# Two blocks on one core: VectorE takes the drain of the latent keys and the last nine low halves of the weights

## What is computed

```python
kvb = (rmsnorm(ckv, kv_a_norm[l]) @ w_kv_b[l]).reshape(B, S, N_HEADS_B, KV_HEAD_B)
k_nope, v_b = kvb[..., :QK_NOPE], kvb[..., QK_NOPE:]
...
x = x + rmsnorm(merged @ w_out[l], post_norm_mix[l])
h2 = rmsnorm(x, pre_norm_mlp[l])
y = jnp.square(jax.nn.relu(h2 @ w_up[l])) @ w_down[l]
x = x + rmsnorm(y, post_norm_mlp[l])
```

## Time and profile before

| | |
|---|---|
| runs, us | 1471.33, 1473.10, 1473.85; median 1473.1 |
| the profiled execution, us | 1473.38 |
| its span in the profile, us | 1471.5 |
| mean granted TensorE clock | 0.965 of full |
| busy: TensorE, VectorE, ScalarE, GpSimd | 90%, 65%, 34%, 34% |
| latent keys | 1097.0 to 1104.3 us of the span |
| up and down stage | about 1277 to 1459 us of the span |

### The profile page before, as it was taken

One profiled execution on the slowest core, in us unless ns is written; L12 is line 12 of the kernel. 1 busy time (PEld: TensorE's weight loads), 2 busy tenths in 40 slices (PEclk: granted clock), 3 DMA queues, 4 the chain that ended last, 5 costly groups with the idle time before them and its releaser, 6 DMA issues.

```text
span 1471.5 us, 25626 instructions
## 1 busy us (share of the span) xinstructions
PE 1317.9 (90%) x9926; PEld 1253.8 (85%) x9926; DVE 955.8 (65%) x2100; ACT 497.2 (34%) x974; POOL 496.9 (34%) x334
## 2 busy tenths in 40 slices
PE   6999999999998886887878886888899999989997
PEld 5999999989888886887868886878776889889997
DVE  4679987665658685859585859655325447683574
ACT  4633456444133121212112121211236455434341
POOL 1588722000224554453535353555012000022221
PEclk9999999999999999898999898999999999999998
DMA  6555554553488999999999999999830125245451
GB/s 244 212 188 185 176 187 166 184 177 154 165 343 329 426 427 427 428 427 427 428 426 426 426 427 427 427 428 427 337 143 29 58 86 194 94 157 199 160 191 40
DMA packets 58090, 397.43 MB, mean 270 GB/s; under 512 B 6288, under 2 KB 9872, under 8 KB 10384
## 3 DMA queue, kind: packets, MB, share of 16 engines
q0 software_dynamic: 36864, 268.45, 43.6%
q1 hardware_dynamic: 21136, 127.76, 24.3%
HBM read 395.14 MB, written 1.05 MB: 269 GB/s over the span
## 4 chain that ended last, share of the span: by engine, by line
PE 55%; DMA 20%; DVE 14%; issue 7%; ACT 3%; POOL 1%; DVEq 0%; POOLq 0%; ACTq 0%
DMA rows_late<-peer_uv_dram,stage 20%; PE bank L721 10%; PE bank L723 10%; PE bank L722 10%; PE bank L963 7%; PE bank L689 6%; PE bank L707 5%; DVE rows_late L1990 4%; ACT w_hi L1165 2%; PE bank L838 1%; DVE w_lo L524 1%; DVE hid L2174 1%; PE bank L862 1%; DVE probs L1916 1%; DVE probs L1914 1%
## 5 line engine op out<-in xcount | busy, mean ns | idle before, releaser
L963 PE MATMUL bank<-h_norm,rows_late 128*128 128x128 f32 x2816 | 329.2, 280 | 24.8 <-ACT h_norm L1352 24.8
L963 PEld LDWEIGHTS bank<-h_norm,rows_late 128*128 128x128 f32 x2816 | 325.6, 196 | 27.8 <-ACT h_norm L1352 27.8
L524 POOL TENSOR_TENSOR w_lo<-raw,w_hi 128x2048 fp32r<-128x2048 f32 x37 | 172.1, 4652 | 392.7 <-ACT w_hi L1165 392.7
L1990 DVE SCALAR_TENSOR_TENSOR rows_late<-rows_late,squares 128x1024 f32<-128x1024 f32 x176 | 213.5, 1229 | 121.1 <-DMA rows_late<-peer_uv_dram,stage 120.6
L963 PE MATMUL bank<-h_norm,rows_early 128*128 128x128 f32 x1280 | 171.9, 300 | 84.7 <-ACT h_norm L1352 84.7
L963 PEld LDWEIGHTS bank<-h_norm,rows_early 128*128 128x128 f32 x1280 | 166.0, 214 | 90.6 <-ACT h_norm L1352 90.5
L631 POOL DMA_INDIRECT rows_late<-peer_uv_dram,stage x165 | 196.4, 1190 | 133.1 <-PE bank L963 94.5
L1165 ACT ACTIVATE w_hi<-raw 128x2048 fp32r<-128x2048 f32 x94 | 178.9, 1904 | 60.4 <-PE bank L723 49.4
L524 DVE TENSOR_TENSOR w_lo<-raw,w_hi 128x2048 fp32r<-128x2048 f32 x57 | 133.0, 2336 | 100.1 <-ACT w_hi L1165 96.5
L721 PE MATMUL bank<-x_hi_a,w_hi 128*128 128x256 f32 x672 | 190.9, 284 | 2.7 <-DVE x_lo_a L1560 1.8
L722 PE MATMUL bank<-x_lo_a,w_hi 128*128 128x256 f32 x672 | 190.2, 283 | 0.0
(11 more groups left out here) (338 smaller groups left out, 2036.5 us busy)
## 6 DMA issues: line engine op xcount, KB each, us to landing
raw<-w_in_dram SPq DMA_DIRECT2D x28, 1024.0 KB, 4.9
raw<-w_up_dram SPq DMA_DIRECT2D x16, 1024.0 KB, 4.9
raw<-w_down_dram SPq DMA_DIRECT2D x16, 1024.0 KB, 4.9
rows_late<-w_in_dram SPq DMA_DIRECT2D x10, 1024.0 KB, 13.4
raw<-w_kv_dram SPq DMA_DIRECT2D x8, 1024.0 KB, 4.8
rows_late<-w_peer_q_dram SPq DMA_DIRECT2D x5, 1024.0 KB, 12.0
raw<-sc_w_out_dram SPq DMA_DIRECT2D x4, 1024.0 KB, 4.8
raw<-cf_w_pw_dram SPq DMA_DIRECT2D x4, 1024.0 KB, 4.8
```

Source lines behind the costliest of these rows:

```text
L524: api.tensor_tensor(ring(w_lo, i), ring(raw, i), ring(w_hi, i).bitcast(F32), ALU.subtract).then_inc(w_lo_ready[LO_BY[i][0]], 1)
L963: mm = nc.tensor.matmul(ct(Y_ACC[c][t // 4], t % 4, P), expert_rows(k)[:, D + t * P:D + (t + 1) * P], ct(diag, k % DIAGS, P), start=False, ...
L1990: w_.scalar_tensor_tensor(out=row, in0=row, scalar=1.0, in1=h_tok[:, c * D:(c + 1) * D], op0=ALU.mult, op1=ALU.mult, accum_out=pre[:, side ...
```

## The change

The eight latent key tiles are drained by VectorE, in its own step 1 behind `inverse_sums(0)`, and no longer by ScalarE. The plan's entry says so, so that the waits on their banks look at VectorE's count. TensorE gets one more wait in step 4 (all `kn` drained). `BY_DVE` now reaches to the last load, so the nine low halves are VectorE's, and GpSimd has no more to do behind the biases of the first eight heads.

```diff
@@ plan() @@
         elif i == 1:
-            p.append(("w_kv_b_2", 0, [("kn", h) for h in range(HB)], "act"))
+            p.append(("w_kv_b_2", 0, [("kn", h) for h in range(HB)], "dve"))
@@
-BY_DVE = range(LOAD_OF["k", 0], LOAD_OF["up", 6])
+BY_DVE = range(LOAD_OF["k", 0], len(LOADS))
@@ block.tensor, beside_attention @@
                 elif i == 4:
                     latent_queries(range(HB // 2, HB))
+                    wait_drained(pe, "kn", HB - 1)
@@ block.scalar, beside_attention @@
-                elif i == 1:
-                    for h in range(HB):
-                        wait_tile(act, "kn", h)
-                        s.activation(ct(k_b, h)[0:NOPE, :], acc("kn", h)[0:NOPE, :], ACT.Copy).then_inc(acc_freed["act"], 1)
@@ block.vector, beside_attention @@
-                if i == 3:
+                if i == 1:
+                    for h in range(HB):
+                        wait_tile(dve, "kn", h)
+                        freed(w_.tensor_copy(ct(k_b, h)[0:NOPE, :], acc("kn", h)[0:NOPE, :]))
+                elif i == 3:
```

## The result

With the change the kernel takes 1476.62 us (median of 19 runs, 1473.43 to 1478.05). The kernel before, run beside it, takes 1472.84 us (19 runs, 1470.41 to 1474.73). The ratio is 1.0024, 95% interval 1.0018 to 1.0031: slower by 3.8 us, 2.6 to 4.6. A second comparison of the same two kernels, further down, gave 1.0015 (1.0005 to 1.0025). The loss is small but real.

What follows compares the result with a forecast made beforehand. TensorE, busy 90% of the span, was taken as the bound, so its waits count. Terms -2.9 + 1.2 + 1.1 + 1.6 = +1.0 us on the profiled 1473.38; against the median, 1474.0 us, range 1470.0 to 1477.5.

Steps and rivals of the forecast that it cites:

- signs of being right: Up stages and first down load: low halves 6.6 us apart, VectorE unheld, 2.5 to 3 us gap, then clock 0.5.
- rival C: Keys and both waits ahead of the down loads: lower clock at all of them, so slower, 1477.5 us; chance 0.12.
- Keys: Latent key tiles: VectorE's copies start TensorE's second batch 1.2 us earlier, at full clock; 2.9 us gained.
- GpSimd's five covered low halves: Down 3, 6, up 1, down 2, 5: moved to VectorE, covered by TensorE's work on the load before; cost nothing.
- The ring: Up 5, down 0; up 4, 7: VectorE and ScalarE alternate, 6.62 us a turn; halves end 1.2 and 1.1 us later.
- The wait of 2.7 us in down 0: First half's first down load: TensorE idles for `hid_lo` before hidden tile 13; lower clock behind it costs 1.6 us.
- The second half's wait: Ahead of the second half's down loads: about 1.6 us plus 0.9; lower clock left out of sum, put into range.
- A: Up and down stage: GpSimd waits and lower clock go, keys give 2.9; 7.8 us faster, 1465.3 us; chance 0.07.

Runs made afterwards that it cites:

- e1: Kernel before with only the drain of the latent keys moved to VectorE, GpSimd keeping its nine low halves: ratio to before 0.9984.
- e4: Keys on VectorE plus five low halves (down 3, 6 of first half; up 1, down 2, 5 of second), against the kernel before: ratio 0.9978.
- e5: Whole change plus filling matmuls on TensorE in its waits inside each half's first down load: ratio to the kernel before 1.0004, stage 185.16 us.
- e3: Keys on VectorE plus four low halves (up 5, down 0 of first half; up 4, 7 of second), against the kernel before: ratio 1.0013.
- e2: Kernel before with only the nine low halves moved to VectorE, ScalarE still draining the keys: ratio to before 1.0029.
- e9: The whole change measured once more, nothing else altered, against the kernel before: ratio 1.0015.
- e6: Whole change, with VectorE taking a load's low half behind the drains of two tiles, not ahead: 1462.29 us, ratio to the kernel before 0.9920.
- e7: As e6, but GpSimd keeps its nine low halves: ratio to the kernel before 0.9950, stage 179.16 us.
- e10: e6 plus nine two-input GpSimd operations on data nobody reads: ratio to the kernel before 0.9941, stage 177.66 us.
- e11: e6 plus nine one-input GpSimd operations on data nobody reads: ratio to the kernel before 0.9950, stage 177.79 us.
- e8: The kernel before profiled again, unchanged: up and down stage 182.87 us, keys to up stage 180.66 us.

## Why the prediction was right, and where it was short

The measured 1476.62 us lies in the range of 1470.0 to 1477.5. The forecast of 1474.0 was 2.6 us too low, and the change turned out slower by a little more than the 0.2% to which I had given 0.67 as no change; for slower I had given 0.19. The signs of being right all came: low halves 6.62 us apart, no VectorE instruction held, a wait of 2.6 us inside down 0 with the clock at 0.50 behind it. That the range still held the result is in part luck. Its upper end was that of rival C, of which one half came true (the lower clock behind both waits) and the other did not (the keys kept theirs), and up to 1.5 us of the measured loss is explained by nothing in the prediction.

- **Keys, forecast 2.9 us gained.** Measured 3.0 in the first pair of profiles (179.53 to 176.49), and 2.4 us in e1's comparison, whose interval of 0.4 to 4.4 us holds the forecast. The wait of 0.9 us kept the clock, as taken from the earlier trace rows.
- **GpSimd's five covered low halves, cost nothing.** e4: 0.00 us.
- **The ring, +1.2 and +1.1 us.** Measured 39.76 and 39.75 us for six turns against the 39.72 forecast, 2.4 us in e5. Right, and on the four loads it named (e3). But 1.2 us is a difference of two pairs that went opposite ways, which the prediction did not say. In the first half of the kernel before, the low halves on both sides of GpSimd's two loads were

```profile
1298.67 2.28 DVE L524 TENSOR_TENSOR w_lo<-raw,w_hi 128x2048 fp32r<-128x2048 f32 x1
1305.27 2.29 DVE L524 TENSOR_TENSOR w_lo<-raw,w_hi 128x2048 fp32r<-128x2048 f32 x1 [1.82 <-ACT w_hi L1165]
```

The pair of loads with up 5 took 1287.20 to 1298.67, 11.47 us, and the pair with down 0 took 1305.27 to 1319.14, 13.87 us, against 13.24 for two turns of the ring. GpSimd's share saved 1.8 us in one pair and cost 0.6 in the other; the second half shows the same, 13.86 and 11.52 us. No run moved one of the four alone.
- **The wait of 2.7 us in down 0, and 1.6 us for the lower clock behind it.** The longest was 2.6 us, and the clock fell; 1.5 us by e5, as half of two.
- **The second half's wait left out of the sum.** This is the term that was mis-sized: "about 1.6 us plus 0.9, between the sizes that kept the clock and those that lost it". The waits were 1.63 and 0.64 us, close to that, and the clock fell to 0.50 behind them in both profiles of the change, in e2 and in e3. This costs another 1.5 us. With it the sum is -3.0 + 2.4 + 2.9 = +2.3 us, 1.0016, which is what the second comparison gave (1.0015) and lies just under the first one's interval (1.0018 to 1.0031).
- What the first comparison shows above that, up to 1.5 us, has no row. The part ahead of the keys varies by more than that, and e9 came out without it; chance is likely, but not shown.
- Two sums are off by a little and change nothing: 1473.1 + 1.0 is 1474.1 and not 1474.0, and C adds 3.3 us where two stretches of 1.6 us are 3.2.

Of the rivals, A's premise was right and its conclusion wrong: VectorE is no longer held, which saves it up to 4.2 us at a time, but the ring set the pace, and its six turns came out 1.2 us longer all the same. The Trainium skill (GPSIMD Engine Reference, Engine selection) advises VectorE for elementwise work; the trace agrees on the durations, and e6 against e7 shows the advice paying 4.7 us once the order allows it. The Trainium skill (GPSIMD Engine Reference, Key points) also says that GpSimd shares its SBUF interfaces with VectorE, with contention for instructions with two SBUF inputs: the rows agree, `hid` at 3.4 to 4.6 us instead of 0.42.

## What to carry to other kernels

Before moving work from a slow side engine to a faster main one, look for a ring: an engine that idles in front of each such piece (here 1.83 us, released by ScalarE) is not short of time but waits its turn, and each load whose piece moves in then takes a full turn (here 6.62 us; a pair of loads with one piece on GpSimd had taken 11.5 to 13.9). Put the piece behind the work that the others wait for; that was worth 13.6 us of stage here, against the 5.3 us that the move alone had cost. And an idle wait on TensorE can cost another 1.5 us in clock behind it: those of 2.1 us and more that are shown here did, and so did 1.6 and 0.6 us in a row; those of 2.0 us (e10, e11) did not. Count a wait near that size with it, or fill it.

## What I had not expected of the hardware

- An elementwise operation of GpSimd with one SBUF input held a VectorE instruction with two SBUF inputs as long as one with two inputs did: 3.40 against 3.37 us for a 0.42 us instruction. By GpSimd's own records its operations lasted 5.4 and 3.7 us there, so the hold did not follow their length.
- The clock fell behind two shorter waits in a row in the second half (TensorE busy for 0.74 of 3 us from 1417 to 1420), not only behind single ones of 2.1 and 2.6 us; with 13 filling matmuls in them it stayed at 1.00. Behind single waits of 1.98 and 2.01 us in e10 and e11 it stayed at 1.00 too.
- The stretch of lower clock behind the same 2.10 us wait differs between executions: 3.4 us in two profiles of the kernel before, 6.8 us in the third (e8).
